# Where the modulation vectors of a two-block model are computed: tensor engine, or three other engines through the head

## The reference

```python
for l in range(DEPTH):                      # 2 layers
    m_lat = jnp.split((jax.nn.silu(c) @ ada_w[l] + ada_b[l])[:, None, :], 6, axis=-1)
    m_ctx = jnp.split(jax.nn.silu(c_ctx) @ ada_w[l] + ada_b[l], 6, axis=-1)
    h = modulate(rmsnorm(x, norm_mix[l]), m_lat[0], m_lat[1])
    hc = modulate(rmsnorm(ctx, norm_mix[l]), m_ctx[0], m_ctx[1])
    ...                                     # projection, fourier, pooling and attention branches
    x = x + m_lat[2] * merge(yf, yp, ya, gates, w_out[l])
    ...                                     # the same for ctx, unless it is the last layer
    h2 = modulate(rmsnorm(x, norm_ffn[l]), m_lat[3], m_lat[4])
    x = x + m_lat[5] * peer(h2, peer_wq[l], peer_keys[l], peer_u[l], peer_v[l])
    ...                                     # the same for ctx, unless it is the last layer
```

## Time and profile before

| what | value |
|---|---|
| median of three runs | 3956.7 us (3955.21 to 3958.97) |
| the profiled execution | 3959.59 us, of which the profile's span is 3957.8 us |
| head (start to the first gather) | 0 to 487 us |
| expert stages, first to last gather issue | 487 to 1316, 1317 to 2122, 2365 to 3075 us |
| second block | 3083 us to the end |
| busy in the span | PE 75%, DVE 61%, ACT 18%, POOL 37% |
| DMA traffic | 1081 MB, mean 273 GB/s |

### The profile page before, as it was taken

One profiled execution on the slowest core, in us unless ns is written; L12 is line 12 of the kernel. 1 busy time (PEld: TensorE's weight loads), 2 busy tenths in 40 slices (PEclk: granted clock), 3 DMA queues, 4 the chain that ended last, 5 costly groups with the idle time before them and its releaser, 6 DMA issues. The chain is left out here.

```text
span 3957.8 us, 31262 instructions
## 1 busy us (share of the span) xinstructions
PE 2957.7 (75%) x8957; PEld 1464.0 (37%) x8957; DVE 2428.0 (61%) x5464; ACT 700.6 (18%) x1849; POOL 1465.3 (37%) x1541
## 2 busy tenths in 40 slices
PE   8898765768778665856587866087448899889987
PEld 1544632214442113213223454022212547564655
DVE  0243577987796558987755357998885256123632
ACT  0212100221122001310132211032013114011311
POOL 0000065674557545765572006677677000000000
PEclk9999887986899878988798988598779999999999
DMA  9242399997999999999996239999999521324212
GB/s 324 78 144 75 102 399 389 405 369 262 395 350 395 360 401 380 406 365 351 379 410 228 77 121 405 411 400 367 408 410 409 210 97 64 126 84 155 73 64 80
DMA packets 359716, 1081.26 MB, mean 273 GB/s; under 512 B 32048, under 2 KB 38652, under 8 KB 358780
## 3 DMA queue, kind: packets, MB, share of 16 engines
q0 software_dynamic: 221184, 805.40, 52.2%
q1 hardware_dynamic: 138364, 273.87, 19.5%
HBM read 1073.92 MB, written 5.24 MB: 273 GB/s over the span
## 5 line engine op out<-in xcount | busy, mean ns | idle before, releaser
L1673 POOL DMA_INDIRECT lent<-in_peer_u_dram,picks_u x308 | 288.9, 938 | 750.3 <-POOLq L367 486.1
L1622 PE MATMUL psum<-lent,heads 128*128 128x512 f32 x616 | 344.9, 651 | 177.5 <-ACT heads L1606 131.1
L1606 ACT ACTIVATE heads<-common,dots 128x128 f32<-128x128 f32 x768 | 296.4, 399 | 707.1 <-PE psum L1622 564.1
L1572 DVE SCALAR_TENSOR_TENSOR lent<-lent,psum 128x1024 f32<-128x1024 f32 x308 | 366.5, 1218 | 64.2 <-DMA lent<-in_peer_u_dram,picks_u 59.7
L789 PE MATMUL psum<-ring,turned 128*128 128x512 f32 (+1 forms) x832 | 345.0, 576 | 61.9 <-PEq L367 35.3
L1673 POOL DMA_INDIRECT lent<-in_peer_v_dram,picks_u x308 | 301.7, 980 | 124.1 <-issue 48.4
L1209 PE MATMUL psum<-ring,turned 128*128 128x512 f32 x512 | 244.5, 639 | 70.6 <-DMA ring<-in_w_in_dram 61.4
L1580 DVE SCALAR_TENSOR_TENSOR psum<-lent,dots,psum 128x512 f32<-128x512 f32 x306 | 230.7, 754 | 93.6 <-DMA lent<-in_peer_v_dram,picks_u 78.8
L1673 POOL DMA_INDIRECT proj<-in_peer_u_dram,picks_u x154 | 145.4, 944 | 355.3 <-POOLq L367 249.9
L1622 PEld LDWEIGHTS psum<-lent,heads 128*128 128x128 f32 x616 | 97.2, 192 | 424.3 <-DMA lent<-in_peer_v_dram,picks_u 271.6
L789 PEld LDWEIGHTS psum<-ring,turned 128*128 128x128 f32 x832 | 164.8, 200 | 237.1 <-issue 206.5
(11 more groups left out here) (300 smaller groups left out, 4878.9 us busy)
## 6 DMA issues: line engine op xcount, KB each, us to landing
ring<-in_w_in_dram SPq DMA_DIRECT2D x37, 2048.0 KB, 8.3
ring<-in_ada_w_dram SPq DMA_DIRECT2D x20, 2048.0 KB, 18.6
ring<-in_w_out_dram SPq DMA_DIRECT2D x10, 2048.0 KB, 8.0
ring<-in_peer_wq_dram SPq DMA_DIRECT2D x10, 2048.0 KB, 8.8
lent<-in_w_in_dram SPq DMA_DIRECT2D x9, 2048.0 KB, 7.8
lent<-in_ada_w_dram SPq DMA_DIRECT2D x4, 2048.0 KB, 12.8
lent<-in_w_out_dram SPq DMA_DIRECT2D x4, 2048.0 KB, 7.6
ring<-in_w_mk_dram SPq DMA_DIRECT2D x4, 2048.0 KB, 14.2
```

Of the source, the lines that this page charges most:

```text
L1572: dve.scalar_tensor_tensor(out=src, in0=src, scalar=1.0, in1=kept_row, op0=ALU.mult, op1=ALU.mult, accum_out=weight).then_inc(rows_used.se ...
L1606: act.activation(diags[n % DIAGS], ident, ACT.Copy, scale=dots[:, j:j + 1]).then_inc(diag_ready.sem, 1)
L1622: pe.matmul(kept_row[:, 0:512], diags[n % DIAGS], row_slot(r)[:, 0:512], start=j == 0, stop=j == PICKS - 1).then_inc(pe_rows.sem, 1)
L1673: pool.indirect_dma_start(out=row_slot(r), out_offset=None, in_=tables_dram[which], in_offset=bass.IndirectOffsetOnAxis(ap=picks_u[:, t, j ...
```

## The change

Layer 0's first four blocks of `ada_w` (shift and scale of the first norm) stay on PE in a shortened `ada_stage`, without its gate products. The remaining eight of layer 0 and all twelve of layer 1 are computed by a class `ModulationSums` that is a host through the head, in place of None. A row is one 128 x 512 piece of a block: for a block with two streams DVE multiplies it by one column of silu(c) and adds it to an accumulator; ACT scales it in place by the other column; POOL adds that to the second accumulator. With one stream DVE has nothing to do. POOL issues the loads, 1 MB for four rows, into two slots that the head doesn't use (`proj` and `heads`), each when its own adds on that slot are through. When a block's eight rows are summed, PE adds over the partitions with four or eight products by a column of ones, into banks 6 and 7. So the head's stages now have six banks: the merge is three units deep, not four, attention two, not three, and three places get waits for banks. Rows are placed by `advance` at a pace for each stage.

Layer 0's missing modulation is finished in a new stage, `rest_of_modulation`, between the late merge and the output product; layer 1's is kept in `soft` (`keep_second_modulation`, after the search) and used by a new guest, `second_modulation`, in place of `ada_stage(1)`. The layer-0 gates of the expert sums become a guest of the first expert stage (`expert_gates`). The small loads get a semaphore of their own, awaited by SP in the norm's stage. Layer 1's early merge is split in two, and the rotation goes after the first part.

```diff
+ADA_FIRST, ADA_BLOCKS = 4, 12
+ROWS_OF_FIRST = 8 * (ADA_BLOCKS - ADA_FIRST)
...
-    def plan_ada(l):
-        for b in range(12):
-            plan_block(("ada", l, b), io["ada_w"][l], 512 * b, 512 * b + 512)
+    def plan_ada():
+        for b in range(ADA_FIRST):
+            plan_block(("ada", 0, b), io["ada_w"][0], 512 * b, 512 * b + 512)
     def plan_w_in(l):
         for b, (c0, c1) in enumerate(((0, 512), (512, 1024), (1024, 1280))):
...
+    def hosted():
+        return host[0] and host[0].block
     def run_vector(vector, dve):
         for us in vector(dve) or ():
...
+    def run_with_sums(work, tensor, vector, scalar, sync):
+        work.marks = [(0, work.row)]
+        with nc.Block(no_gpsimd_drain=True) as block:
+            @block.vector
+            def _(dve):
+                if vector:
+                    products.watch = work.mark
+                    run_vector(vector, dve)
+                    products.watch = None
+                while work.row < work.target:
+                    work.vector_sums(dve)
+            @block.tensor
+            def _(pe):
+                work.tensor_sums(pe, work.marks[0][1])
+                for n in (tensor(pe) or () if tensor else ()):
+                    work.tensor_sums(pe, work.rows_before(n) - (12 if work.row <= ROWS_OF_FIRST else 4))
+                if work.target:
+                    work.tensor_sums(pe, work.row)
+            @block.scalar
+            def _(act):
+                for n in (scalar(act) or () if scalar else ()):
+                    work.scalar_sums(act, work.rows_before(n))
+                work.scalar_sums(act, work.row)
+            @block.gpsimd
+            def _(pool):
+                work.pool_sums(pool)
             @block.sync
             def _(sp):
...
-        yield sp.dma_start(tables[:, 0:3584], io["first"]).then_inc(*loaded.one(16))
+        yield sp.dma_start(tables[:, 0:3584], io["first"]).then_inc(*small_loaded.one(16))
...
+    def await_small(sp):
+        sp.wait_ge(*small_loaded.now())
...
+            turn(pe, ADA_FIRST - 1)
...
+            dve.wait_ge(*products.at(2 * ADA_FIRST))
+            n = 4 * ADA_FIRST
+            chain(dve, step_v, dve.tensor_tensor(
+                out=mods_v[:, 0:n, :], in0=psum[:, turned_bank, 0:2 * n].rearrange("p (j s) -> p j s", s=2),
+                in1=ada_bias(0, 0, n, 2), op=ALU.add))
+            make_gain(dve, 0, 0, 2)
...
+    class ModulationSums:
+        def __init__(self):
+            self.block = None
+            self.blocks = [(0, b) for b in range(ADA_FIRST, ADA_BLOCKS)] + [(1, b) for b in range(ADA_BLOCKS)]
+            self.width = [2 if l == 0 or b < ADA_FIRST else 1 for l, b in self.blocks]
+            self.count = 8 * len(self.blocks)
+            self.row = self.row_pe = self.row_act = self.row_pool = self.loads = self.target = 0
+            self.owed, self.pace = 0.0, None
+            self.marks = []
+            self.slots = [v.rearrange("p (k n) -> p k n", k=4) for v in (proj[:, 7168:9216], heads[:, 0:2048])]
+            self.landed = [signal(f"modulation_landed{i}") for i in range(2)]
+            self.first_steps, self.scaled = signal("modulation_first"), signal("modulation_scaled")
+            self.added, self.summed = signal("modulation_added"), signal("modulation_summed")
...
+        def await_load(self, eng, row):
+            half = row // 4
+            eng.wait_ge(self.landed[half % 2].sem, 16 * (half // 2 + 1))
...
+        def advance(self, dve, us):
+            if self.pace is None:
+                return
+            self.owed += us
+            while self.row < self.limit and self.owed >= self.pace:
+                self.owed -= self.pace
+                self.vector_sums(dve)
+        def host(self, stage, pace=None, target=0, limit=None):
+            self.owed, self.pace, self.target = 0.0, pace, target
+            self.limit = self.count if limit is None else limit
+            stage()
+        def vector_sums(self, dve):
+            i, k = divmod(self.row, 8)
+            if self.width[i] == 2:
+                if k % 4 == 0:
+                    self.await_load(dve, self.row)
+                acc, w = self.partial(i, 0), self.weights(self.row)
+                if k == 0:
+                    self.await_place(dve, i)
+                    dve.tensor_scalar(acc, w, cond[:, k, 0:1], None, ALU.mult).then_inc(self.first_steps.sem, 1)
+                else:
+                    dve.wait_ge(self.first_steps.sem, self.firsts(self.row))
+                    dve.scalar_tensor_tensor(out=acc, in0=w, scalar=cond[:, k, 0:1], in1=acc, op0=ALU.mult, op1=ALU.add)\
+                       .then_inc(self.first_steps.sem, 1)
+            self.row += 1
+        def scalar_sums(self, act, stop):
+            while self.row_act < stop:
+                i, k = divmod(self.row_act, 8)
+                last = self.width[i] - 1
+                if last:
+                    act.wait_ge(self.first_steps.sem, self.firsts(self.row_act + 1))
+                elif k % 4 == 0:
+                    self.await_load(act, self.row_act)
+                if k == 0:
+                    self.await_place(act, i)
+                w = self.weights(self.row_act)
+                act.activation(self.partial(i, last) if k == 0 else w, w, ACT.Copy,
+                               scale=cond[:, k, last:last + 1]).then_inc(self.scaled.sem, 1)
+                self.row_act += 1
+        def pool_sums(self, pool):
+            while self.row_pool <= self.row:
+                if self.row_pool % 4 == 0:
+                    self.load(pool)
+                if self.row_pool == self.row:
+                    break
+                i, k = divmod(self.row_pool, 8)
+                if k:
+                    pool.wait_ge(self.scaled.sem, self.row_pool + 1)
+                    if k > 1:
+                        pool.wait_ge(self.added.sem, self.adds(self.row_pool))
+                    acc = self.partial(i, self.width[i] - 1)
+                    pool.tensor_tensor(out=acc, in0=self.weights(self.row_pool), in1=acc, op=ALU.add)\
+                        .then_inc(self.added.sem, 1)
+                self.row_pool += 1
+        def load(self, pool):
+            while self.loads < min(2 * len(self.blocks), self.row_pool // 4 + 2):
+                h = self.loads
+                l, b = self.blocks[h // 2]
+                if h >= 2:
+                    pool.wait_ge(self.added.sem, self.adds(4 * (h - 1)))
+                src = io["ada_w"][l][512 * (h % 2):512 * (h % 2) + 512, 512 * b:512 * b + 512]
+                pool.dma_start(self.slots[h % 2], src.rearrange("(k p) n -> p k n", p=P)).then_inc(self.landed[h % 2].sem, 16)
+                self.loads += 1
+        def tensor_sums(self, pe, row):
+            while 8 * (self.row_pe + 1) <= row:
+                i = self.row_pe
+                l, b = self.blocks[i]
+                pe.wait_ge(self.first_steps.sem, self.firsts(8 * i + 8))
+                pe.wait_ge(self.added.sem, self.adds(8 * i + 8))
+                for s in range(self.width[i]):
+                    for c in range(4):
+                        j = 2 * (4 * b + c) + s
+                        mm = pe.matmul(psum[:, 6 + l, j:j + 1], self.partial(i, s)[:, c * P:c * P + P], ones[:, 0:1],
+                                       start=True, stop=True)
+                mm.then_inc(self.summed.sem, 1)
+                self.row_pe += 1
+    def gates_of(gate_list, row0=0):
+        diag = [soft[:, 128 * i:128 * i + 128] for i in range(3)]
+        def tensor(pe):
+            for i in range(len(gate_list)):
+                if i % 4 == 0:
+                    yield 0
+                pe.wait_ge(*ready_v.at(i + 1))
+                pe.matmul(psum[:, i // 4, 128 * (i % 4):128 * (i % 4) + 128], ones, diag[i % 3],
+                          start=True, stop=True).then_inc(*products.one())
+        def vector(dve):
+            for i, (w, s, k) in enumerate(gate_list):
+                if i >= 3:
+                    dve.wait_ge(*products.at(i - 2))
+                dve.tensor_scalar(diag[i % 3], ident, mods_v[:, 8 * (2 + 3 * w) + k, s:s + 1], None, ALU.mult).then_inc(*ready_v.one())
...
+    def rest_of_modulation(sums):
+        open_stage()
+        tensor, gates, scalar = gates_of(gate_entries(0, range(2)))
+        def vector(dve):
+            dve.wait_ge(sums.summed.sem, ADA_BLOCKS - ADA_FIRST)
+            chain(dve, step_v, dve.tensor_tensor(
+                out=mods_v[:, 16:48, :], in0=psum[:, 6, 32:96].rearrange("p (j s) -> p j s", s=2),
+                in1=ada_bias(0, 16, 48, 2), op=ALU.add))
+            gates(dve)
+            make_gain(dve, 0, 1, 2)
+        run_stage(tensor, vector, scalar)
...
+    def second_modulation():
+        open_stage()
+        tensor, gates, scalar = gates_of(gate_entries(0, range(1)) + gate_entries(1, range(1)))
+        def vector(dve):
+            for j0, j1, ns in ((0, 16, 2), (16, 48, 1)):
```

(38 more changed lines are left out.)

165 lines of the change are left out of this document (97 added, 68 removed).

## The result

The changed kernel takes 3931.9 us (median of 7 runs, 3926.4 to 3942.7), the kernel before, on the same chip, 3959.0 (3955.2 to 3967.9). The ratio is 0.9931, interval 0.9916 to 0.9946: 27 us less, where 71 were forecast (3886 us, with a range of 3850 to 3933). The profiled execution took 3930.23 us, its span 3928.4, against 3959.59 before.

The account below looks back on a forecast made before the run. The head was taken as bound by TensorE, the expert stages by DMA. Head -11, first expert stage +3 and second -63 gave -71 us: 3956.7 to 3886, range 3850 to 3933.

Parts of the forecast that it names:

- The modulation stage: Head's first stage: eight of twelve blocks leave; norm begins near 57.5 us, since the barrier waits for SP: -57 (-50 to -66).
- The second expert stage: Layer 1's modulation leaves it, 25.2 MB less to load: 743 us against 806.5, -63 (bounds -45 and -75).
- the first quarter: Second expert stage's first 128 gathers: 203.1 us, as in the first expert stage, plus 8 for gates and norm: 211.
- The prices: Sums in the head: DVE step 0.69 us, ACT scaling 0.60, POOL add 1.2, POOL load 1.5, landing 5.1.
- Rival 2: Head: POOL's load issue is dear, 3.8 us, 2.1 us a row; 39 us more, 3925 in all; chance 15%.
- The head: All stages before the expert stages: modulation's saving less the costs of sums, products and new stages: -11 us.
- PE's products: 128 one-column products across the head, 1.6 us per two-stream block; PE is the bound, so they count: +18 (0 to 25).
- 63 fits in 97.9: Merge: 37 rows at 1.7 us take 63 us, within the stage's 97.9; +3 of PE stalls for rotation on three banks.
- 27 in 43.4 fits: Attention: 16 rows at 1.7 us take 27 us, within the stage's 43.4.
- The attention: Head stage bound by PE: DVE goes from 23.9 us to 35 of 43, costing +2.
- rival 3: Head: DVE steps and POOL adds exclude each other, 1.9 us a row; projection +5, merge +7, attention +9: 3907; chance 20%.
- keys (+10): Keys stage: 49 rows need 76 us, some 5 loaded ahead, in 62 us; ACT's rows precede copies that release PE: +10.

## Why the prediction was right or wrong

*The modulation stage* (-57, measured -59.8). Right, with its reason: SP is last into the barrier. Its small loads came at 0.45 us apiece at the end, not 1.0.

*The second expert stage* (-63, measured -76.6; over three traces of before and three of after, all on chips of about 3957 us, -70 to -77). Right in kind, near its lower bound of -75. The term mis-sized is the first quarter, 211 against 200.6: the 8 us put down for gates and norm weren't there. Third 180.8 for 188, fourth 178.6 for 171.3.

*The prices.* POOL's addition 1.25 us at its shortest (1.2 forecast), its load 0.77 (1.5, and even the lower bound of 0.94 was too high), landing 5.6 to 6.3 (5.1), ACT's scaling 0.72 (0.60), DVE's step 0.75 (0.69). Rival 2, the dear issue, is out. A row by these prices alone would be no dearer than forecast.

*The head* (-11, measured +38.3). This is what failed: 49 us. By the terms below 30 of them are clock, 10 stalls and 9 PE's products; the rest (modulation -3, new stages +2, topk +4, others) about cancels. The step was the comparison of rows times 1.7 us with the stage's length ("63 fits in 97.9", "27 in 43.4 fits"). It treats the rows as a stream with a capacity of its own. The rows did fit; what they did to PE is what costs, and the terms were these:

1. The granted clock, 30 us, for which the prediction had no term and no rival. Just ahead of each stretch at 1.2 GHz PE either stood idle (from 117.7, after its wait from 115.0 to 122.2 had begun; from 203 and 251, after 2.5 and 3.9 us) or did one-column products (from 271 and 336, after both; from 309, after one block's 16 instructions from 305.6 to 307.5, with no idle time). The attention (+2 forecast for the stage, +13.9 measured) is all this but for 1.9 us of products. With the additions gone, and nearly all stalls with them, 12 us are left; with seven of eight products gone, and stalls of 42 us, 29. So the clock's part goes with the stalls more than with the products. That a given stall brings a given stretch wasn't separated, and in the attention the additions make no difference that stands out of the scatter (clock 0.85 without them, 0.77 three times and 0.85 once with them).
2. Stalls, 30 us, against some 20 forecast (projection 3, merge 3, attention 2, late merge 2, keys 10). They come from POOL's additions (3 are left without them) in three ways. Shared access, rival 3 at 21 us and 20%, is there: 11 to 24 us with its share of the clock. Its place was other than priced (projection 5, merge 7, attention 9): 13 in the merge, none seen in the projection (51.9 with additions and with writes of the same length), and in the attention PE stalls no more than before (1.2 us for 1.3), though TENSOR_SCALAR is held up (797 ns for 487). The length of POOL's chain is 22 us, with its clock: keys (+10) and projection (+3) were forecast for it, and the projection came out at +7.9. The place in line is 6 us: ACT's scalings behind tanh, so that loads came late and rows bunched with the rotation.
3. PE's products, +18 forecast. The price was near (0.115 us an instruction for 0.10), 27 us of PE, some 12 on the path by the estimate from one trace. The place was wrong: five blocks and 8 us in the merge, where three blocks came and lie in stalls, and none in the branches, where the products of two blocks left from the projection stand at the start (x32, 7 us, at the lower clock): +9.7.

The merge's 29 us: 13 go with the shared access (127 to 114 beside writes of the same length), 6 with ACT's line, each shown by one edit; about 9 stay without any addition (106.7 against 97.9), 5.5 of them PE's products by the count. Whether the three add up wasn't tested: the length of POOL's work is in the gap between 114 and 106.7 too.

The sum, against the profiled executions: -71 forecast, +49 in the head, -14 in the second expert stage, -2 in the first, +8 in what follows, which makes the 29 measured. What follows isn't touched by the change, yet it took 1828.8, 1830.3 and 1828.6 us in three traces before and 1836.6, 1830.3 and 1840.2 after. Part of it is the third expert stage (736.5 to 737.1 us before, 739.3 to 741.9 after), and in one trace the stretch ahead of it (243 us for 233 to 235); why is open.

The measured 3931.9 us lies 1 us inside the range (3850 to 3933). That is luck: its upper end was the dear issue of rival 2, which is out, and the clock, the largest single term of the miss, wasn't in it.

By the Trainium skill (SBUF — State Buffer, Who interferes with whom) tensor_scalar can enter a two-port mode and then contends with GpSimd too, and PE and ACT never wait on anyone. The trace agrees: 797 ns for 487 on DVE, 696 beside POOL's writes, and ACT's scaling is at 0.718 us with POOL adding, writing or without its additions. It would not have given rival 3 a larger price, since the attention lost nothing by it.

## What to carry to other kernels

Work spread over idle engines isn't priced by capacity: list, stage by stage, behind which wait of the host's own each piece stands in its engine's line, and which of the host's operations share an access with it. Where PE was at 98% and a clock of 1.00, give what the spread work does to PE, stalls and small products, a second price for stretches at half clock; here that was as much as the stalls themselves (24 to 35 us for 29 to 32), and it fell to 12 when the stalls were gone. An accumulator in PSUM, and the helper's instructions moved ahead of the host's waits, recovered 12 of the merge's 29 us with a few lines. Time the scatter of the unchanged kernel first: a head that moves by 13 us by itself can't judge an edit worth 10, but a stage that repeats within 2 can.

## What the runs showed of the hardware

- A 1 MB load issued by POOL in 512 pieces of 2 KB occupies POOL for 0.77 us, less than a gather of 128 rows (0.94).
- Even DVE operations of 128x2 numbers are held up by an addition on POOL: a TENSOR_SCALAR on `stats` that takes 0.17 us alone had a mean of 1.2 us over two in the merge of the version with the sum in PSUM.
- POOL's writes hold up a DVE TENSOR_SCALAR of 128x512 in SBUF (696 ns on average for 487), but not a step with two operands in SBUF (0.75 us beside them).
- PE's one-column products, each with a fresh 128x128 weight load, cost 0.115 us an instruction at full clock: 1.84 us for a block of two streams, and about 3.5 at 1.2 GHz (3.97 for 18 instructions).
- The granted clock of one stage isn't the same in every run: the attention of the changed kernel had 0.77 three times (57.3 us) and 0.85 once (52.7 us).
- The same kernel took 3959 us in one set of runs and 4169 in another, 5% more. By two traces of the changed kernel all of it lies in stages that gather: 830 and 895 us for the first expert stage, 861.7 and 856.8 for the second block.
